# A PEER layer's last 32 tokens taken off TensorE: expert rows gathered and worked off on VectorE, and the last output stage with stationary weights

## What is computed

```python
q = (tb @ wq).reshape(PEER_BLOCK, PEER_HEADS, 2, PEER_HALF)       # 8 heads
s = jnp.einsum('thpd,hpnd->thpn', q, keys)                        # 2 x 128 keys a head
sv, si = lax.top_k(s, PEER_TOPK)                                  # 16 of each half
comb = (sv[:, :, 0, :, None] + sv[:, :, 1, None, :])...           # 256 pairs
fv, fi = lax.top_k(comb, PEER_TOPK)                               # 16 pairs a head
eidx = ...                                                        # i * 128 + j, one of 16384 experts
gate = jax.nn.softmax(fv, axis=-1)
hid = jax.nn.gelu(jnp.einsum('td,thkd->thk', tb, jnp.take(u_tab, eidx, axis=0)))
return jnp.einsum('thk,thkd->td', gate * hid, jnp.take(v_tab, eidx, axis=0))
```

## Time and profile before

| | |
|---|---|
| median of 3 runs | 2359.24 us (2359.15 to 2362.71) |
| profiled execution, first to last instruction | 2347.2 us |
| what lies around that span, by the median | 12.0 us |
| TensorE busy, weight load, VectorE | 92%, 88%, 58% |
| ScalarE, GpSimd | 44%, 46% |
| DMA, mean over the span | 136 GB/s |
| mean granted TensorE clock | 0.958 |

### The profile page before, as it was taken

The page is one execution under the profiler, slowest core; times in us unless marked ns, Lnnn a source line. Parts: engine busy times, 40 slices in busy tenths (PEclk is TensorE's granted clock), DMA queues, the critical chain, the costliest instruction groups (busy, mean ns, idle before and its releaser), DMA issues.

```text
span 2347.2 us, 46712 instructions
## 1 busy us (share of the span) xinstructions
PE 2170.2 (92%) x17280; PEld 2058.2 (88%) x17280; DVE 1369.6 (58%) x2698; ACT 1031.7 (44%) x1670; POOL 1071.2 (46%) x537
## 2 busy tenths in 40 slices
PE   7856799999999999999998677999999999999999
PEld 6855799999999999999988656898999999888887
DVE  2873319964677755555546744169627776555555
ACT  4412346664333344444444222466663333444444
POOL 4794367886666500000026971578876665000000
PEclk9977899999999999999999768999999999999999
DMA  4200244444444455555544001354554444555555
GB/s 149 89 2 1 72 162 145 165 158 142 134 134 134 135 170 171 177 171 177 171 142 143 1 1 36 127 171 162 170 165 140 143 143 133 189 188 189 190 191 172
DMA packets 87784, 320.09 MB, mean 136 GB/s; under 512 B 9744, under 2 KB 10000, under 8 KB 87312
## 3 DMA queue, kind: packets, MB, share of 16 engines
q1 hardware_dynamic: 87696, 318.91, 41.0%
HBM read 317.82 MB, written 1.05 MB: 136 GB/s over the span
## 4 chain that ended last, share of the span: by engine, by line
PE 57%; POOL 23%; issue 18%; DVE 1%; ACT 0%; POOLq 0%; DMA 0%; SPq 0%; DVEq 0%
PE ps L790 57%; POOL w_lo L502 14%; POOL arena L523 5%; POOL arena L532 3%; DMA w<-w_c 0%; POOLq L508 0%; DVE h L1613 0%; DVE x L1225 0%; POOLq L501 0%; DVE x L1605 0%; DVE x_lo L1218 0%; POOL arena L519 0%; DVE sel L1517 0%; ACT arena L598 0%; DVE onehots_j L1213 0%
## 5 line engine op out<-in xcount | busy, mean ns | idle before, releaser
L502 POOL TENSOR_TENSOR w_lo<-w,w_hi 128x1024 fp32r<-128x1024 f32 x344 | 858.8, 2506 | 902.3 <-ACT w_hi L580 902.1
L790 PE MATMUL ps<-x_hi,w_hi 128*128 128x272 f32 (+1 forms) x4768 | 1178.7, 290 | 33.0 <-POOL w_lo L502 19.7
L790 PE MATMUL ps<-x_hi,w_lo 128*128 128x272 f32 (+1 forms) x3744 | 1073.1, 287 | 0.0
L790 PEld LDWEIGHTS ps<-x_hi,w_hi 128*128 128x128 f32 x4768 | 835.2, 189 | 40.5 <-POOL w_lo L502 24.6
L580 ACT CAST w_hi<-w 128x1024 fp32r<-128x1024 f32 x596 | 623.4, 1046 | 437.1 <-DMA w<-v_c 386.7
L790 PE MATMUL ps<-x_lo,w_hi 128*128 128x272 f32 (+1 forms) x2720 | 775.2, 285 | 0.0
L790 PEld LDWEIGHTS ps<-x_hi,w_lo 128*128 128x128 f32 x3744 | 706.0, 189 | 0.0
L790 PEld LDWEIGHTS ps<-x_lo,w_hi 128*128 128x128 f32 x2720 | 514.4, 189 | 0.2
L1587 DVE TENSOR_TENSOR w_lo<-w,w_hi 128x1024 fp32r<-128x1024 f32 x252 | 308.8, 1225 | 335.9 <-ACT w_hi L580 335.9
L790 PE MATMUL ps<-w_hi,x_hi 128*128 128x512 f32 x1024 | 319.2, 393 | 0.0
L790 PE MATMUL ps<-arena 64*64 64x64 f32 (+7 forms) x2432 | 179.1, 282 | 84.0 <-ACT arena L695 19.4
(11 more groups left out here) (159 smaller groups left out, 1674.8 us busy)
## 6 DMA issues: line engine op xcount, KB each, us to landing
w<-u_c SPq DMA_DIRECT2D x256, 512.0 KB, 3.3
w<-v_c SPq DMA_DIRECT2D x256, 512.0 KB, 3.3
w<-w_c SPq DMA_DIRECT2D x84, 512.0 KB, 3.3
arena<-keys_c SPq DMA_DIRECT2D x2, 1024.0 KB, 6.3
arena<-mix_c SPq DMA_DIRECT2D x2, 632.0 KB, 6.8
h<-h SPq DMA_DIRECT2D x1, 1088.0 KB, 5.0
out<-x SPq DMA_DIRECT2D x4, 256.0 KB, 2.1
arena<-lora_c SPq DMA_DIRECT2D x2, 256.0 KB, 7.0
```

The lines of the kernel that those rows point to most:

```text
L502: g.tensor_tensor(wlo_t[:, slot], wraw_t[:, slot], whi_t[:, slot].bitcast(F32), ALU.subtract).then_inc(s_lo, 1)
L790: return nc.tensor.matmul(out_, lhsT, rhs, start=start, stop=stop, skip_group_check=True)
```

## The change

In both layers the last 32 of the 272 tokens (`NG`) are taken out of stages 1 to 3. Their normed input is repeated four times over the 128 partitions (`xs_rep`: 32 tokens x 4), so that every partition stands for one token and 32 of its 128 chosen experts. GpSimd gathers the chosen rows of `u` and then of `v` by indirect DMA, 32 gathers of 128 rows of 4 KB each per table and layer, through three slots (`ROWS`). VectorE takes a dot product with each `u` row and, after GELU and gate, sums the `v` rows. A product with `fold` on TensorE adds the four partial sums of a token into the output banks, before the last output tile. These VectorE operations stand between the weight and activation parts of stage 3, at the tiles of `DOT_AT` and `SUM_AT`.

The moving width becomes 240 in layer 0 and 224 in layer 1, `steps` 60 and 56, `split` 68 and 72, `quiet` 64 and 48. Layer 1's output stage takes the form of layer 0's (24 products with stationary weights, 224 columns); the residual products at its start go; at the end `h` is added as in layer 0, and 16 transposes on TensorE, two copies each on ScalarE and VectorE, and four stores write it. VectorE's part of stage 3 is written out instead of looped.

```diff
+NG = 32
+TG = T - NG
+REP = P // NG
+SLOTS = PH * TOPK // REP
+ROWS = 3
+DOT_AT = [3 + 7 * m // 4 for m in range(SLOTS)]
+SUM_AT = [64 + 7 * m // 4 for m in range(SLOTS)]
+GELU_AT = 60
...
-        self.steps = self.nt // OHT
+        self.nd = self.nt - (NG if l in GATHERED else 0)
+        self.by_rows = self.last and l not in GATHERED
+        self.steps = self.nd // OHT
...
                 lows(l, NZ + AHEAD, NP)
+                if LAYERS[l].gathers is not None:
+                    pool.wait_ge(s_ix, LAYERS[l].gathers + 1)
+                    for k in range(2 * SLOTS):
+                        n = 2 * SLOTS * LAYERS[l].gathers + k
+                        if n >= ROWS:
+                            pool.wait_ge(s_rf, n - ROWS + 1)
+                        g.indirect_dma_start(
+                            rows[n % ROWS], None, tables[k // SLOTS],
+                            bass.IndirectOffsetOnAxis(g_idx[:, k % SLOTS:k % SLOTS + 1], 0)).then_inc(s_row[n % ROWS], 16)
...
+                if L.gathers is not None:
+                    act.wait_ge(s_xr, L.gathers + 1)
+                    nc.scalar.copy(xs_rep[:, 0:HALF], ps[:, 7, :])
+                    nc.scalar.copy(xs_rep[:, HALF:D], ps[:, 0, :]).then_inc(s_xrc, 1)
...
+                first = GELU_AT if L.gathers is not None else 0
+                if first:
...
+                    act.wait_ge(s_rf, 2 * SLOTS * L.gathers + SLOTS)
+                    nc.scalar.activation(g_dot, g_dot, ACT.Gelu_apprx_tanh).then_inc(s_gg, 1)
...
+                if L.last and not L.by_rows:
+                    for b in (0, 2):
+                        act.wait_ge(s_ot, b // 2 + 1)
+                        nc.scalar.copy(done_t[:, b * HALF:(b + 1) * HALF], ps[:, b, :]).then_inc(s_don[0], 1)
...
+                if L.gathers is not None:
+                    pe.wait_ge(s_xd, L.gathers + 1)
+                    for c in range(DC):
+                        last = mm(ps[:, 7 if c < 4 else 0, c % 4 * P:(c % 4 + 1) * P],
+                                  xs_rep[:, c * P:(c + 1) * P], ident, True, True)
+                    last.then_inc(s_xr, 1)
                 pe.wait_ge(s_keys, 16 * (l + 1))
...
-                    project(l, NU0 + i, L.t0, it, 1 + i % UB)
+                    project(l, NU0 + i, L.t0, it, 1 + i % UB, L.nd)
...
+                if L.gathers is not None:
+                    s, r = len(L.tiles) - 1, slice(P - NG, P)
+                    for q in range(REP):
+                        last = mm(ps[NG * q:NG * (q + 1), 0, 3 * P:3 * P + 3 * SLOTS].rearrange("p (m n) -> p m n", m=3),
+                                  ident[r, r], chosen[r, s, :, SLOTS * q:SLOTS * (q + 1)], True, True)
...
-                            last = mm(ps[:, c, 0:L.nt], a[:, slot, c, :], b, i == 0 and k == 0, True)
+                            last = mm(ps[:, c, 0:L.nd], a[:, slot, c, :], b, i == 0 and k == 0, True)
...
+                    if i == NKEYS - 1 and L.gathers is not None:
+                        pe.wait_ge(s_rf, 2 * SLOTS * (L.gathers + 1))
+                        for c in range(DC):
+                            mm(ps[:, c, L.nd:L.nt], g_sum[:, c * P:(c + 1) * P], fold, False, True)
                     output(i)
+                if L.last and not L.by_rows:
+                    for b in (0, 2):
+                        for c in range(2 * b, 2 * b + 4):
+                            pe.wait_ge(s_hd, DC * l + max(c + 1, 2))
+                            for tt in range(2):
+                                t = L.t0 + tt * P
+                                last = nc.tensor.transpose(ps[:, b + tt, c % 4 * P:(c % 4 + 1) * P], h[:, c, t:t + P],
+                                                           ident)
+                        last.then_inc(s_ot, 1)
...
+                if L.gathers is not None:
+                    dve.wait_ge(s_xl, (3 * l + 3) * DC)
+                    v.tensor_tensor(xs_rep.rearrange("p (c q t) -> p c q t", c=DC, q=REP),
+                                    bc(xh[:, :, TG:T].bitcast(F32), 2, REP), bc(xl[:, :, TG:T].bitcast(F32), 2, REP),
+                                    ALU.add).then_inc(s_xd, 1)
...
+                def expert_dot(m):
+                    r = landed(m)
+                    v.tensor_tensor_reduce(r, r, xs_rep, 1.0, 0.0, ALU.mult, ALU.add,
+                                           g_dot[:, m:m + 1]).then_inc(s_rf, 1)
+                def expert_sum(m):
...
+                        v.scalar_tensor_tensor(g_sum, r, g_dot[:, m:m + 1], g_sum, ALU.mult, ALU.add).then_inc(s_rf, 1)
...
+                if L.gathers is not None:
+                    for i in range(AHEAD, NKEYS):
+                        weight_low(i)
+                        act_low(i)
+                        if i in DOT_AT:
+                            expert_dot(DOT_AT.index(i))
+                        if i in SUM_AT:
+                            expert_sum(SUM_AT.index(i))
```

More of the change, by code:

```diff
@@ L251, in trunk @@
         done_t = xn_t[:, 0:len(BLOCKS) * HALF]
-        hid = [arena_t[:, 0:P * L.nt].rearrange("p (i t) -> p i t", i=P) for L in LAYERS]
+        hid = [arena_t[:, 0:P * L.nd].rearrange("p (i t) -> p i t", i=P) for L in LAYERS]
+        assert max(P * L.nd for L in LAYERS if L.gathers is not None) <= P * T - (ROWS + 1) * D
+        rows = [arena_t[:, P * T - (ROWS + 1 - b) * D:P * T - (ROWS - b) * D] for b in range(ROWS)]
+        xs_rep = arena_t[:, P * T - D:P * T]
+        g_sum = xs_rep
+        g_gate, g_at, g_dot = sel[:, 0, TG:T], sel[:, 1, TG:T], sel[:, 2, TG:T]
+        g_idx = g_at.bitcast(U32)
+        tables = ur_c, v_c.rearrange("l i p d -> (l i p) d")
         def res(name):
@@ L428, in trunk @@
         s_out = sem("output_stored")
+        s_xd = sem("gathered_tokens_x_replicated")
+        s_xr = sem("gathered_tokens_x_in_psum")
+        s_xrc = sem("gathered_tokens_x_copied")
+        s_ix = sem("expert_rows_indexed")
+        s_row = [sem(f"expert_row_landed_{b}") for b in range(ROWS)]
+        s_rf = sem("expert_row_consumed")
+        s_gg = sem("gathered_hidden_gelu")
+        s_don = [sem(f"done_block_ready_{e}") for e in ("act", "dve")]
+        s_ot = sem("output_transposed")
         s_dl = sem("dve_link")
@@ L770, in act_high @@
                     act.wait_ge(s_use, l * NW + NV0 + i - UB + 1 + WR * it)
-                    nc.scalar.copy(act_hi[:, i % UB, 0:L.nt],
+                    nc.scalar.copy(act_hi[:, i % UB, 0:L.nd],
                                    hid[l][:, bass.ds(WR * it + i, 1), :].squeeze(1)).then_inc(s_ah, 1)
@@ L776, in _ @@
                     act_high(i)
-                with act.Fori(0, NKEYS // WR - 1) as it:
+                first = GELU_AT if L.gathers is not None else 0
+                if first:
+                    with act.Fori(0, first // WR) as it:
+                        for j in range(WR):
+                            high(l, NV0 + j + AHEAD, it)
+                            act_high(j + AHEAD, it)
+                    act.wait_ge(s_rf, 2 * SLOTS * L.gathers + SLOTS)
+                    nc.scalar.activation(g_dot, g_dot, ACT.Gelu_apprx_tanh).then_inc(s_gg, 1)
+                with act.Fori(0, (NKEYS - first) // WR - 1) as it:
                     for j in range(WR):
-                        high(l, NV0 + j + AHEAD, it)
-                        act_high(j + AHEAD, it)
+                        high(l, NV0 + first + j + AHEAD, it)
+                        act_high(first + j + AHEAD, it)
                 for i in range(NKEYS - WR, NKEYS):
@@ L1165, in output @@
                     last.then_inc(s_use, 1)
-                if L.last:
+                if L.by_rows:
                     for b, (tt, hh) in enumerate(BLOCKS):
@@ L1613, in _ @@
                     v.tensor_tensor(hc, hc, ps[:, c, 0:L.nt], ALU.add).then_inc(s_hd, 1)
+                if L.last:
+                    for b in (1, 3):
+                        dve.wait_ge(s_ot, b // 2 + 1)
+                        v.tensor_copy(done_t[:, b * HALF:(b + 1) * HALF], ps[:, b, :]).then_inc(s_don[1], 1)
+                    continue
                 dve.wait_ge(s_hd, DC * (l + 1))
```

90 lines of the change are left out of this document (62 added, 28 removed).

## The result

The changed kernel takes 2319.01 us (median of 4 runs, 2316.66 to 2320.51), the kernel before 2359.19. The ratio is 0.9821, 95% interval 0.9807 to 0.9835: 40 us faster, where 89 were forecast.

What follows compares the result with a forecast made beforehand. TensorE was taken as the bound (92% busy), waiting in the first stage for GpSimd's low parts of the weights. Layer 0's -66.6 and layer 1's -22.2 us took 2359.2 to 2270, range 2250 to 2295 (80%: 2212 to 2330).

Steps and rivals of the forecast that it cites:

- The price of narrow products: TensorE products of 240 and 224 columns take 112 ns each, 2.69 us a tile in both layers.
- A: Rival: no floor under the narrow TensorE products, 110 and 103 ns each; 2219 us in all; chance 14%.
- B: Rival: narrow TensorE products have a floor at 117 ns, what 256 columns cost; 2319 us in all; chance 13%.
- Stage 2: Hidden tiles with gate products: eight steps fewer per layer, 3.56 us each; -49.6 us in layer 0, -36.1 in layer 1.
- Stage 1: Hidden tiles alone, beside VectorE's ranking: more tiles, +17.3 us in layer 0 and +20.4 in layer 1, start included.
- Stage 3: Output tiles: narrower products and mostly hidden gathers; -35.1 us in layer 0, -9.8 in layer 1.
- (c): Output tiles' weight loads have 2.0 us of slack; only operation plus gather exceed it, costing 4 us and 3 us.
- the end: After layer 1's last output products: adds, 8 transposes, a copy and the store, +2.5 us with hops.
- (a): Output tiles' DMA: a tile and 4/7 of a gather need 306 GB/s, against 409 in the saturated first stretch; hidden.
- C: Rival: gathered rows slower than 4.7 us each set the output tiles' pace; 2437 us at 6 us a row; chance 8%.
- D: Rival: VectorE is full in the output tiles, an expert operation taking 2.2 us; +47, 2317 us; chance 7%.
- E: Rival listed with a chance of 4%; the prediction's text gives neither its claim nor its size.

Runs made afterwards that it cites:

- small rows: Changed kernel with each gather bringing 128 of 1,024 columns (64 KB, not 512 KB), VectorE's expert operations staying about as long: 2257.04 us.
- short operations: Changed kernel with whole gathers, but VectorE's expert operations covering 8 of 1,024 columns: 2337.20 us.
- layer 1 alone: Changed kernel with only layer 1 gathering, layer 0 as before the change: 2362.61 us, ratio 1.0027 to the kernel before.

## Why the prediction was wrong, step by step

**The price of narrow products: right.** 112 ns were taken for 240 and 224 columns, 112.0 and 111.6 measured, and the floor reaches down to 32 columns. Rivals A and B, 110/103 and 117, are out. The 117 ns themselves were misread: 214 counts products that are cut by the window's edges, and the spacing there is 118. It enters neither layer's sum.

**Stage 2: right.** 214.9 us for 60 steps are 3.58 each, 197.4 for 56 are 3.53 (forecast 3.56); -48.6 and -37.9 against -49.6 and -36.1.

**Stage 1: right in its making, too low by 3.7 and 7.4 us.** The start cost 2.2 us in each layer (forecast 2.5). GpSimd's tiles while the ranking runs and behind it:

```profile
374.13 2.37 POOL L521 TENSOR_TENSOR w_lo<-w,w_hi 128x1024 fp32r<-128x1024 f32 x1 [13.27 <-ACT w_hi L609]
...
535.45 2.39 POOL L521 TENSOR_TENSOR w_lo<-w,w_hi 128x1024 fp32r<-128x1024 f32 x1 [1.82 <-ACT w_hi L609]
...
1512.80 2.36 POOL L521 TENSOR_TENSOR w_lo<-w,w_hi 128x1024 fp32r<-128x1024 f32 x1 [10.06 <-ACT w_hi L609]
...
1652.56 2.37 POOL L521 TENSOR_TENSOR w_lo<-w,w_hi 128x1024 fp32r<-128x1024 f32 x1 [1.68 <-ACT w_hi L609]
...
1690.23 2.38 POOL L521 TENSOR_TENSOR w_lo<-w,w_hi 128x1024 fp32r<-128x1024 f32 x1 [2.05 <-ACT w_hi L609]
...
1701.93 2.38 POOL L521 TENSOR_TENSOR w_lo<-w,w_hi 128x1024 fp32r<-128x1024 f32 x1 [2.01 <-ACT w_hi L609]
```

In layer 1 the 44 tiles from 2 to 46 take 139.8 us, 3.18 each, where 3.08 was forecast and 3.16 was the pace: narrower products gained nothing there, 4 us of the miss. The free loops take 11.70 us (11.2 forecast, 11.49 before), 2.9 a tile: some 3 us. The forecast had put the loops before 0.2 to 0.3 us over the sum of their chain; by its own terms, with 3.01 and 2.81 for the tile, they were 0.89 and 0.45 over. In layer 0 the 52 tiles to 535.45 take 161.3 us against 165.8, a gain of 4.5 of the 6 expected; what took the other 2 us behind them wasn't looked into.

**Stage 3: the step that failed is the slack, (c).** The forecast said of an operation (1.2 to 1.4 of 2.0 us) and a gather (up to 1.28) that "only both together break through, by half a microsecond: 4 us for layer 0, 3 for layer 1 (bounds 0 and 20)". Measured, as the difference to the kernel with small rows: 14.9 and 23.0 us in layer 0, 29.7 and 36.8 in layer 1, in the two executions of the changed kernel. With those removed, 345.9 and 353.1 us remain, where the forecast without its stalls has 346.3 and 351.1. So the rest of stage 3 was right, the end among it (from the last product to the end 6.0 us, before 3.2). TensorE's idle time alone shows only 9.3 and 19.7 us of the loss; the counts show all: 2729 products in 320 us against 2858 with small rows are 14 us at 112 ns, 2825 in 345 against 2867 in 320 are 30. Two things in (c) were wrong. It needed operation and gather together, and the gather alone does it (short operations: 377.4 and 388.4). And it let a gather hold a load back by its own transfer, 1.28 us, where landing and slack, 3.3 + 2.0 = 5.3 us, were overrun by 23 and 39 loads, by up to 2.0 and 2.5 us. The average in (a), 306 GB/s of 409, was near (284 and 272 measured) and said nothing of it: a slack of 2 us is used up by single loads, not by the mean.

The Trainium skill (DMA: Bandwidth & Descriptors, Queues, rings and completion order) says that each DMA engine goes round the queues that it has work for, one packet at a time. The late load above agrees: at its end the packets of the two queues alternate one for one, 0.155 us apart. Other loads weren't taken apart in this way.

**The rivals.** C: no row set VectorE's pace; among its waits in the output stages there is none for a gather. D: an expert operation takes 1.22 us (and 0.08 for reading the sum) or 1.28, not 2.2. E: the fast rate stays down to 32 columns; what fell while the narrow ones ran was the granted clock. The time, 2319, is rival B's figure and 2 us from rival D's 2317, by chance in both cases.

The expert operations in layer 0's output stage, by line and form (count, busy us, mean ns):

```profile
L1696 DVE SCALAR_TENSOR_TENSOR arena<-arena,sel 128x1024 f32<-128x1024 f32 x31 | 39.6, 1278 | 0.0
L1683 DVE CUSTOM_DVE_ANT_0 arena<-arena 128x1024 f32<-128x1024 f32 x30 | 36.5, 1218 | 0.0
L1683 DVE DVE_READ_ACCUMULATOR2_ANT sel<- 128x1 f32 x30 | 2.5, 82 | 0.0
```

**What stays open.** The changed kernel's output stages vary by 7 to 9 us from one execution to the next (360.8 and 368.9, 382.8 and 389.9; 373.6 with layer 1 alone), its stages 1 and 2 by up to 3 us, more than the 1 us expected of them. Part of it is the clock: the mean granted clock of output 1 is 1.00 with small rows, 0.99 in the execution of 382.8 us and 0.97 in that of 389.9. So part of what is called stalls here is time at the 1.2 GHz level; that the stalls bring the clock down is likely, not shown. Why layer 1 stalls more than layer 0 at the same price of a tile wasn't tried. Why one DMA engine would fall behind the others isn't known. Moving half of the gathers into stage 2, where the DMA share is 0.45, wasn't tried either.

## What to carry to other kernels

Bandwidth that fits on average doesn't protect a short prefetch ring: put the latest arrival of a single load against the slack, with every other transfer that can be in flight beside it, before costing new DMA traffic at nothing. Where a load waits for the last use of its buffer, look at which instructions read that very buffer, and let them come first: some 30 us here for another order of products. And split a change by layer before judging it: here one layer gave all, and the other nothing until the loads started earlier.

## What the runs showed of the hardware

- Back-to-back fp32r products, each with its own load of 128 stationary columns, take at least 112 ns at the 2.4 GHz level (32, 192, 224 and 240 columns alike) and 213 ns at the 1.2 GHz level (64, 128 and 192 columns). In the kernel's output stages it is 112 ns as well. That the load is what sets it is likely, but no run varied the stationary side.
- The granted clock fell to 0.50 at about 2350.5, after a stream of 32-column products 112 ns apart, stayed there through those of 64 and 128 columns, and was back at 1.00 at about 2377.7, while 192-column products ran. By the profile TensorE was busy all the time, so a stream without gaps can still be granted the lower level.
- An indirect gather of 512 KB occupies GpSimd for 0.93 us at least at its issue, with a median of 0.94 for `u` and 1.68 for `v`, and up to 3.4. Whole rows with short operations stall TensorE no less than with long ones (377.4 against 360.8 and 368.9). That rows which are given back sooner bring the next gather sooner may be the reason; it isn't shown.
- The 16 parts of one 512 KB load don't end together when gathers run beside it: in the load looked at 14 had ended 3.6 us after the issue, the last 7.3 us after it.
